# Neighbourhood attention with the values stationary in TensorE, the output feature-major, and the weights scaled before they are turned

## The reference, cut to what matters

```python
def neighbourhood_attention(q, k, v, rel_bias):
    ...
        s = jnp.einsum('bhcd,bhicjd->bhcij', q_row, k_win).astype(jnp.float32) * scale + bias[None]
        p = jax.nn.softmax(s.reshape(B, H, GRID_W, kh * kw), axis=-1).reshape(B, H, GRID_W, kh, kw)
        return jnp.einsum('bhcij,bhicje->bhce', p.astype(v_win.dtype), v_win)
...
def odd_mixer(x, w_qkv, rel_bias, w_o):
    ...
    o = neighbourhood_attention(q.reshape(shp), k.reshape(shp), v.reshape(shp), rel_bias)
    return o @ w_o
```

## Time and profile before

| | us |
|---|---|
| median of 3 runs | 3354.98 (3354.79 to 3358.0) |
| the profiled execution | 3351.62 |
| its span in the trace | 3349.8 |
| the attention stage in it: first scores to first matmul of the output projection | 1201.2 to 1313.7 |

### The profile page before, as it was taken

The page is one execution under the profiler, slowest core; times in us unless marked ns, Lnnn a source line. Parts: engine busy times, 40 slices in busy tenths (PEclk is TensorE's granted clock), DMA queues, the critical chain, the costliest instruction groups (busy, mean ns, idle before and its releaser), DMA issues.

```text
span 3349.8 us, 38937 instructions
## 1 busy us (share of the span) xinstructions
PE 3064.6 (91%) x14639; PEld 2389.3 (71%) x14639; DVE 2164.5 (65%) x2376; ACT 1596.5 (48%) x1889; POOL 397.3 (12%) x274
## 2 busy tenths in 40 slices
PE   8677799999996999699999987998899998999998
PEld 6456667667765878577767755877778887778886
DVE  2375578888885245688888866555467654757753
ACT  2354267777774334377777764442232212732221
POOL 0000212222222000222122221010000000000000
PEclk9898899999998999799999998998999999999999
DMA  7300479899884211499999984330123322223321
GB/s 249 115 1 1 156 294 360 346 347 357 348 344 157 76 45 45 188 350 357 359 345 359 354 295 102 73 76 1 51 76 100 101 101 89 88 82 101 101 96 68
DMA packets 174481, 599.22 MB, mean 179 GB/s; under 512 B 25571, under 2 KB 74899, under 8 KB 124947
## 3 DMA queue, kind: packets, MB, share of 16 engines
q1 hardware_dynamic: 140528, 541.75, 44.2%
q0 software_dynamic: 23472, 51.42, 4.3%
q10 hardware_dynamic: 10355, 4.33, 0.5%
HBM read 581.17 MB, written 48.23 MB: 188 GB/s over the span
## 4 chain that ended last, share of the span: by engine, by line
PE 77%; DMA 7%; DVE 7%; ACT 4%; issue 3%; POOL 1%; DVEq 0%; SPq 0%; POOLq 0%; ACTq 0%
PE bank L1787 22%; PE bank L1789 21%; PE bank L1788 21%; DMA ring<-w_gate 4%; PE bank L2288 2%; PE bank L2053 1%; PE bank L1983 1%; ACT ring_rounded L1242 1%; PE bank L1884 1%; PE bank L1762 1%; PE bank L1860 1%; DVE st L2693 1%; PE bank L2073 1%; PE bank L1931 1%; DMA big<-expert_rows,idx 1%
## 5 line engine op out<-in xcount | busy, mean ns | idle before, releaser
L1788 PE MATMUL bank<-ring_rounded,big_rounded 128*96 128x512 f32 (+1 forms) x1712 | 674.6, 394 | 0.0
L2928 DVE TENSOR_TENSOR ring_rounded<-ring,big_rounded 128x2048 fp32r<-128x2048 f32 x252 | 567.9, 2288 | 39.5 <-ACT big_rounded L1242 37.9
L2583 DVE TENSOR_TENSOR ring_rounded<-ring,ring_rounded 128x2048 fp32r<-128x2048 f32 (+2 forms) x126 | 278.0, 2248 | 412.4 <-ACT ring_rounded L1070 412.2
L1242 ACT ACTIVATE big_rounded<-ring 128x2048 fp32r<-128x2048 f32 x252 | 478.1, 1918 | 62.6 <-DMA ring<-w_up 50.5
L1070 ACT ACTIVATE ring_rounded<-ring 128x2048 fp32r<-128x2048 f32 (+2 forms) x126 | 230.3, 1878 | 456.6 <-DMA ring<-ffn_w_down 162.9
L2928 DVE TENSOR_TENSOR ring_rounded<-ring,ring_rounded 128x2048 fp32r<-128x2048 f32 x128 | 292.8, 2289 | 170.7 <-ACT ring_rounded L1242 162.8
L1787 PE MATMUL bank<-big_rounded 128*96 128x512 f32 x1008 | 401.3, 398 | 0.2
L1789 PE MATMUL bank<-big_rounded,XH_rounded 128*96 128x512 f32 x1008 | 398.4, 395 | 0.0
L1787 PE MATMUL bank<-XT_rounded,ring_rounded 128*128 128x512 f32 x928 | 364.7, 393 | 2.4 <-DVE big L3017 2.4
L1789 PE MATMUL bank<-XT_rounded,ring_rounded 128*128 128x512 f32 x928 | 361.7, 390 | 0.0
L1788 PE MATMUL bank<-XH_rounded,ring_rounded 128*128 128x512 f32 x928 | 361.7, 390 | 0.0
(11 more groups left out here) (423 smaller groups left out, 4546.8 us busy)
## 6 DMA issues: line engine op xcount, KB each, us to landing
ring<-w_up SPq DMA_DIRECT2D x128, 1024.0 KB, 8.0
ring<-w_down SPq DMA_DIRECT2D x128, 1024.0 KB, 7.9
ring<-w_gate SPq DMA_DIRECT2D x128, 1024.0 KB, 7.3
ring<-ffn_w_up SPq DMA_DIRECT2D x44, 1024.0 KB, 6.5
ring<-ffn_w_down SPq DMA_DIRECT2D x10, 2048.0 KB, 7.8
ring<-ret_gdn_w_in SPq DMA_DIRECT2D x8, 2048.0 KB, 13.1
expert_rows<-lnp POOLq DMA_DIRECT2D x1, 12288.0 KB, 39.4
ring<-odd_w_qkv SPq DMA_DIRECT2D x6, 2048.0 KB, 7.9
```

Of the source, the lines that this page charges most:

```text
L1242: act.activation(one_pass(expert_hi(j)), expert_raw(j), ACT.Copy).then_inc(signal("half_rounded").sem, 1)
L1788: pe.matmul(dst, x_hi, y_lo, start=False, stop=False)
L2583: dve.tensor_tensor(one_pass(w), w, parts(hi(c)[:, ks, :]), ALU.subtract).then_inc(split[c.pair], 1)
L2928: dve.tensor_tensor(one_pass(expert_raw(j)), expert_raw(j), parts(expert_hi(j)), ALU.subtract).then_inc(signal("half_split").sem, 1)
```

## The change

- `weighted(i)` swaps the operands. The values (128 keys by 64 features) are loaded as weights and the 128 turned weights move. The output has 64 features in the partitions, head 0 in 0 to 63 and head 1 in 64 to 127, and the band's 128 queries in columns 128b to 128b+127 of one bank. Four steps fill a bank with one whole k-slice of the feature-major output. Only the last of four raises `full`; the others raise a new signal `weighted`.
- All key blocks now have 128 rows. So the unseen half must be zero in the weights: DVE clears the edges with two memsets ahead of step 0 and two ahead of step 12 (L2774 of the changed kernel).
- A query's sum now runs along the free direction of the output, so DVE scales the weights in SBUF before they are turned: L2796, 128x512 numbers for inner bands, 2x192 for edge bands. The turn waits for `p_scaled` where it waited for `exp_done`.
- The weights have four buffers, one for each band (`weights(i)`), in `XH` for the first 12 steps and in `big` after. The bands go 0, 1, 2, 3 in all groups.
- `turn("o1_T")` is gone. ACT rounds a finished group in its turn with i % 4 = 3 (`back_to_grid`), ahead of its copy; DVE writes the remainder at the end of its turns 8, 12, 16 and so on (`rest_from_bands`).
- `keep_busy` ahead of the turn is 128 columns where it was 256, and the one ahead of the weighted product is gone.
- `plan_windows`: scores, turns and `turn_qk` share banks 0 to 5, the outputs alternate between banks 6 and 7.
- The second shifted copy of the values lands where queries of groups 0 to 3 stood, so its DMA waits for the `turn_qk` of group 3. The first load of `odd_w_o` is behind it on SP's queue. POOL's wait for the mixer's norm parameters moves from the first to the last output bank.

```diff
+        def plan_windows(first):
+            groups, banks = C_HEADS // 2, N_BANKS - 2
+            order = (plan.pick(i % banks) for i in itertools.count(first if first < banks else 0))
...
+                if i >= 3 and i % T == 3 and len(U["o1_T"]) < groups:
+                    U["o1_T"].append(plan.pick(banks + len(U["o1_T"]) % 2))
...
+        p_early = XH[:, :, :].rearrange("p t d -> p (t d)")[:, 4 * S:8 * S].rearrange("p (b m s) -> p b m s", b=T, m=2)
+        p_late = big[:, 14336:14336 + 4 * S].rearrange("p (b m s) -> p b m s", b=T, m=2)
...
-            g = i // T
-            return g, ((0, 1, 2, 3) if g == 0 else (3, 0, 1, 2))[i % T]
+            return divmod(i, T)
...
+                    if i == 1:
+                        u = U["C"]["qk"][3][1]
+                        sp.wait_ge(full[u.bank], u.n + 1)
...
                         if i >= 4:
-                            act.wait_ge(full[u["o"][i - 4][0].bank], u["o"][i - 4][0].n + 1)
+                            if i % T == 3:
+                                back_to_grid(i // T - 1)
+                            else:
+                                act.wait_ge(signal("weighted").sem, steps_weighted(i - 4))
...
+            def back_to_grid(g):
+
+                u = U["o1_T"][g]
+                act.wait_ge(full[u.bank], u.n + 1)
+                act.activation(one_pass(by_fours(XT[:, g, :])), from_fours(ps(u)[:, :]), ACT.Copy).then_inc(signal("xt_rounded").sem, 1)
...
-                    keep_busy(v, 256)
-                    pe.wait_ge(signal("exp_done").sem, signal("exp_done").next(pe))
...
-                    keep_busy(v, 128)
-                    pe.wait_ge(drained[u["t"][i][0].bank], u["t"][i][0].n + 1)
...
+                    keep_busy(v, 128)
+                    pe.wait_ge(signal("p_scaled").sem, signal("p_scaled").next(pe))
...
-                    first, second = slice(0, P), slice(0, P)
-                    if b == 0:
-                        second = slice(0, 64)
-                    if b == 3:
-                        first = slice(64, P)
...
-                            ins = pe.matmul(ps(v)[:, C_DIM * m:C_DIM * (m + 1)], C["WT"][rows, i % 2, m, c, :], v_rows, start=(c == 0), stop=(c == 1))
-                    ins.then_inc(full[v.bank], 1)
+                            v_rows = C["V2"][g // 4][:, b - 1 + c, low] if b in (1, 2) else C["H"][:, (0 if b == 0 else 2) + c, 2 * D + cols.start:2 * D + cols.stop]
+                            ins = pe.matmul(ps(v)[C_DIM * m:C_DIM * (m + 1), b * P:(b + 1) * P], v_rows, C["WT"][:, i % 2, m, c, :], start=(c == 0), stop=(c == 1))
+                    ins.then_inc(full[v.bank] if i % T == T - 1 else signal("weighted").sem, 1)
...
-                turn("o1_T", XH, None)
-                mixer_out("odd_o", "o1_T", 1, feature_rows(o_lo_T))
+                mixer_out("odd_o", "o1_T", 1, feature_rows(x_hi_B))
...
+                        if i in (0, 3 * T):
+                            for edge in (weights(i)[:, :, 192:256], weights(i + 3)[:, :, 0:64]):
+                                dve.memset(edge, 0.0).then_inc(dve_done.sem, 1)
+                                dve.wait_ge(dve_done.sem, dve_done.next(dve))
...
-                        dve.tensor_tensor(XH[:, b, P * g:P * g + P].rearrange("p (m d) -> p m d", m=2), ps(v)[:, 0:P].rearrange("p (m d) -> p m d", m=2),
-                                          rep(rcp[:, j:j + 2], 2, C_DIM), ALU.mult).then_inc(drained[v.bank], 1)
...
+                        dve.tensor_tensor(p, p, rep(rcp[:, j:j + 2], 2, p.shape[2]), ALU.mult).then_inc(signal("p_scaled").sem, 1)
+                    if i >= 8 and i % T == 0:
+                        rest_from_bands(i // T - 2)
```

More of the change, by code:

```diff
@@ L289, in plan_attention @@
                     u["o"].append(plan.take(outs))
+        def plan_windows(first):
+            groups, banks = C_HEADS // 2, N_BANKS - 2
+            order = (plan.pick(i % banks) for i in itertools.count(first if first < banks else 0))
+            u = U["C"] = dict(qk=[None] * groups, s=[], t=[])
+            U["o1_T"] = []
+            u["qk"][0] = [next(order), next(order)]
+            for i in range(groups * T + 3):
+                if i < groups * T:
+                    u["s"].append([next(order), next(order)])
+                    if i % T == 2 and i // T + 1 < groups:
+                        u["qk"][i // T + 1] = [next(order), next(order)]
+                if 2 <= i < groups * T + 2:
+                    u["t"].append(next(order))
+                if i >= 3 and i % T == 3 and len(U["o1_T"]) < groups:
+                    U["o1_T"].append(plan.pick(banks + len(U["o1_T"]) % 2))
         def plan_moe(l):
@@ L337, in build @@
             plan.freed[W["qkv"][i].slot] = ("bank", U["qkv"][i][-1])
-        plan_attention("C", C_HEADS // 2, 2, 1)
-        U["o1_T"] = plan.take(KD)
+        plan_windows(U["qkv"][5][T - 1].bank + 1)
         plan.slot = 2
@@ L993, in _ @@
             if on(5):
-                pool.wait_ge(full[U["o1_T"][0].bank], U["o1_T"][0].n + 1)
+                pool.wait_ge(full[U["o1_T"][KD - 1].bank], U["o1_T"][KD - 1].n + 1)
                 norm_params(a["ln1_g"][1], a["ln1_b"][1])
@@ L1962, in weighted @@
                     g, b = band(i)
[L1963 to L1964 removed]
+                    v = U["o1_T"][g]
+                    if i % T == 0 and v.n:
                         pe.wait_ge(drained[v.bank], v.n)
[L1966 to L1967 removed]
+                    pe.wait_ge(drained[u["t"][i].bank], u["t"][i].n + 1)
                     if i in (0, n // 2):
@@ L2744, in windows @@
                 u, n = U["C"], C_HEADS // 2 * T
-                for i in range(n + 3):
+                for i in range(n + 1):
                     if i < n:
@@ new lines, in windows @@
+                    if i >= 8 and i % T == 0:
+                        rest_from_bands(i // T - 2)
+                c = W["odd_o"][0]
+                for i, ks in enumerate(pieces(c)):
+                    w, h = raw(c)[:, ks, :], hi(c)[:, ks, :]
+                    dve.wait_ge(rounded[c.pair], 2 * c.nth - 1 + i)
+                    dve.tensor_tensor(one_pass(w), w, parts(h), ALU.subtract).then_inc(split[c.pair], 1)
+                    if i == 0:
+                        rest_from_bands(C_HEADS // 2 - 1)
```

63 lines of the change are left out of this document (25 added, 38 removed).

## The result

The changed kernel takes **3330.19 us** (median of 4 runs, 3327.89 to 3333.68) against 3354.89 us for the kernel before beside it (4 runs, 3350.14 to 3358.0): 24.7 us less by the medians, whose ratio is 0.9926. The comparison's own estimate of the ratio is 0.9944 with an interval of 0.9925 to 0.9963, so 12 to 25 us less. The forecast was 3341.0, 14.0 less, with a range of 3335 to 3352. A later comparison gave 0.9929 (experiment e10).

The account below looks back on a forecast made before the run. The prediction took PE to bound the attention stage, VectorE and ACT following. Head +0.3, 6.5 groups -10.7 and tail -3.6 sum to -14.0, taking the median from 3354.98 to 3341.0 us, range 3335 to 3352.

Parts of the forecast that it names:

- Groups 10.9 apart, PE still the chain: Attention stage: a group of four steps falls from 12.55 to 10.9 us, with PE still the bound.
- A product of eight passes 0.107 apart: Weighted product: eight fp32 passes of 128 columns cost 0.86 us, 0.97 with the change of tile.
- first rival: Weighted product: column tiles overlap, a product costs 0.75 and a group about 10.4, giving 3337.5 us; chance 0.14.
- No dearer in edge bands: Weighted product: with zero edges and 128-row blocks, edge bands cost as inner ones, removing excesses of 0.61 and 0.31 us.
- A hole of 0.1 behind the turn: Between turn and weighted product: the change to a 128x64 tile shows as a 0.1 us hole, priced at 0.11.
- PE waits for ACT's copy, about 0.5 a group: Ahead of the weighted product: PE arrives earlier and waits for the turned weights, 0.5 us a group, ends 0 and 1.3.
- Full clock from about 1219: Head of the stage: PE's clock is at its full level from about 1219 us on.
- No L1762 row, 13.5 from the last scores to the fifth term: Tail: PE's output transposes vanish and the output projection's fifth term starts 13.5 us after the last scores, -3.6.
- VectorE's price: Scaling of the weights on VectorE: 0.69 us for 128x512, 0.56 for 384; 9.0 us a group, below PE's 10.4.
- weight loads are not hidden: Weighted product: each pass pays 0.15 more in a 128x64 tile, a product costs 2.1, giving 3366 us; chance 0.05.
- the clock: Attention stage: PE at the lower clock, a group costs about 17.5, 25 to 30 us more, 3368 us; chance 0.04.
- The waits eat it: Attention stage: waits cost 1.3 a group or loads are half hidden, group near 12, giving 3350 us; chance 0.17.

Follow-up runs that it names:

- e10: The changed kernel again, unaltered, beside the kernel before on the same chip; 3323.92 us against 3347.8, ratio 0.9929.
- e3: Changed kernel with `keep_busy` ahead of the turn back at 256 columns instead of 128; 3324.51 us, ratio to before 0.9938.
- e1: Changed kernel with head 0's weighted product issued twice, 12 passes where 8 were; 3340.67 us.
- e5: Changed kernel with edge bands using 64-row blocks again for the seen half, the zero edges left unused; 3337.43 us.
- e2: Kernel before with `keep_busy` cut to 128 columns ahead of the turn and removed ahead of the weighted product; 3345.14 us against 3343.24, ratio 1.0.
- e8: Changed kernel with four 512-column `keep_busy` ahead of the first turn and four ahead of the output projection; 3328.26 us.
- e12: Changed kernel with 256-column `keep_busy` ahead of the turn and a 128-column filler matmul ahead of every weighted product; 3323.44 us.
- e7: Changed kernel with ACT's copy of the turned weights moved ahead of `qk_bands` and of the finished group's rounding; 3325.51 us.
- e11: Changed kernel with ACT's copy ahead of `qk_bands` and rounding, plus four 512-column fillers ahead of the output projection; 3316.39 us, ratio to before 0.9908.

## Why the forecast was right in its sign and short in its size

Point by point, in the order of the forecast:

1. **"Groups 10.9 apart, PE still the chain": both halves failed.** 10.13, and the chain runs over VectorE and ACT for most of the groups. e3 shows it: 0.84 us more of PE work cost 0.02.
2. **"A product of eight passes 0.107 apart": the pass was right, the sum was wrong.** The step that failed is the term for the product with its change of tile, 0.86 + 0.11 = 0.97. In the same rows of the chain it is 0.59. The forecast's first rival had the mechanism, tiles that overlap, with one pass of eight saved (0.75). By e1 four of eight are saved. 4 x 0.38 is 1.5 us a group on PE. What misled me was to look at the order of issue (one head after the other) as if it were the order of work. The row that I cited for the rival, four score passes of 256 columns in 0.63, already showed two tiles (of 64 rows) side by side, and I priced it as an exception.
3. **"No dearer in edge bands"**: right, 0.59 and 0.60; with alternating rows an edge product is 1.42 (e5).
4. **"A hole of 0.1 behind the turn"**: right, 0.53 against 0.43.
5. **"PE waits for ACT's copy, about 0.5 a group"**: the place was right, the size was not. The long wait is in the step with i % 4 = 3, for the copy behind `qk_bands` and the exponent, 1.08 us. A faster PE arrives earlier and waits longer, so of the 1.5 us of item 2 nearly half (0.65) came back as waits: 10.9 - 1.5 + 0.65 = 10.1.
6. **"Full clock from about 1219"**: it was back at full at about 1214.9, and 1.00 in the window 1216 to 1218. What had to be weighed was how long it stays low:

```profile
1202.00:1204.00 2.00, 0.05 (x1) 0.00 (x0) 1.97 (x3) 1.39 (x6) 0.00 (x0) 1.00 0.01 4
1204.00:1206.00 2.00, 0.13 (x1) 0.14 (x2) 1.93 (x4) 0.00 (x0) 0.00 (x0) 0.67 0.00 0
1206.00:1208.00 2.00, 2.00 (x9) 1.24 (x9) 1.86 (x6) 0.70 (x3) 0.00 (x0) 0.50 0.00 0
...
1214.00:1216.00 2.00, 2.00 (x16) 1.34 (x14) 0.52 (x3) 0.89 (x3) 0.00 (x0) 0.77 0.00 0
1216.00:1218.00 2.00, 2.00 (x20) 1.33 (x19) 1.86 (x5) 0.88 (x3) 0.00 (x0) 1.00 0.00 0
```

   In these windows of the changed kernel (columns as in e2) the clock falls behind a PE that has done nothing since about 1202 and is low for 10.2 us in all, 3.4 more than before. The forecast had that only as the upper end of its head term (+3) and not in the sum. It took nothing for the gain on the other side, an edge product at half clock of 1.13 where seven passes took 2.33. The gain outweighed the loss: head -3.8 against -0.9, and by e5 3.1 of that hangs on the zero edges. How the other 0.7 arose was not tested.
7. **"No L1762 row, 13.5 from the last scores to the fifth term"**: the transposes are gone. The projection's first matmul starts 10.5 behind the last scores (1280.09 to 1290.59), and ACT's and VectorE's queues ahead of it were foreseen. The fifth term is 1.2 late, at 14.66. The forecast had left out that PE, whose 3.7 us of transposes were gone, would now stand for 3.55 us and lose its clock. With the filler it is 13.3 (e8).
8. **VectorE's price** (0.69 and 0.56 a scaling) was right to the hundredth, and so was that it doesn't become the bound: taken out it gives 0.34 a group.

Of the rivals, "weight loads are not hidden" is excluded by 0.60 for a product, and "the clock" by the granted 1.00 from 1216 until the last product. "The waits eat it" is half true: at 1.15 a group they were near that rival's 1.3, on top of a product that was so cheap that it didn't matter. Two of the rivals' sums have slips that touch neither the forecast nor the range. The overlap's 17.5 adds the head's 0.3 where it should take it off (16.9). The clock's 3368 doesn't follow from its own "25 to 30 more", which is 3380 to 3385.

The sum once more: stage -19.7 against -14.0; of the 5.7 beyond, 3.8 lie in the five groups, 2.9 in the head, 0.2 behind S28, and 1.2 were lost in the tail. The medians differ by 24.7 and in e10 by 23.9, so 4 to 5 us more than the stage. The profiled pair has 3.25 of them ahead of it, where the code is the same. The stage's 19.7 lie inside both intervals (12 to 25 us, and 18 to 29), so these runs don't show that there is anything beyond the stage, nor that there isn't.

## What to carry to other kernels

Price an output that is split into column tiles by the passes in the fuller tile, not by all passes issued (0.60 and 1.07 us here, the second 0.06 more than that); and keep the rows of all blocks alike, even by padding with zeros. When PE gets faster, list at once who becomes late: here reordering two items of ACT's queue, with no instruction removed, made the stage 5.3 us shorter, 3.2 of it in the five groups, where the whole change had brought 12.1. Where a change removes work that filled PE's wait for weights that VectorE and ACT still prepare, try a filler there: it gave 1.4 us here (e8), while both fillers inside the groups cost 3.2 (e12).

## What the hardware showed that I had not expected

- Two 128x64 tiles work side by side in fp32, also where one tile's four passes are all issued ahead of the other's: 8 passes of 128 columns, 4 in each tile, in 0.60 us with the changes of tile; 12 passes, 8 of them in one tile, in 1.07. With eight issued ahead, the second tile began 0.49 later.
- A product whose blocks alternate between 128 and 64 rows costs 1.42 instead of 0.59 us, and 2.50 instead of 1.13 at 1.2 GHz. About half of the 0.83 is that the two tiles no longer overlap.
- The clock can stay at 1.2 GHz under a PE that is never idle: from 1208 to about 1221.4 us in e2, with its fillers cut, where it was low for 20.5 us in all. In the kernel before, with them, it was 6.8 us, in the changed kernel 10.2 in both of its traces, in e3 6.8 and in e12 3.4. These are single traces, and e7 and e11 with the same code have 6.8 and 3.4, so of these differences only the larger ones may be put down to the fillers. A sum of durations doesn't hold them.
